# Expert matrices of a mixture-of-experts layer loaded whole, 2 MB at a time, in place of two halves of 1 MB

## What is computed

```python
def hier_moe(u, w_rg, b_rg, w_re, b_re, w_gate, w_up, w_down):
    g_prob = softmax(xf @ w_rg + b_rg);  g_val, g_idx = top_k(g_prob, 1)      # one of 4 groups
    top_v, top_i = top_k(e_in, MOE_TOPK)                                      # 2 of its 8 experts
    ...
    for g in range(MOE_GROUPS):
        h = silu(einsum('nd,edf->nef', xf, w_gate[g])) * einsum('nd,edf->nef', xf, w_up[g])
        out = out + einsum('nef,ne,efd->nd', h, combine[:, g], w_down[g])
```

## Time and profile before

| | us |
|---|---|
| median of 3 runs | 1304.13 |
| lowest, highest | 1302.29, 1308.63 |
| the profiled execution's own time | 1302.72 |
| its span, first to last instruction | 1300.9 |
| PE busy | 1243.2 |
| DVE busy | 912.5 |
| ACT busy | 682.3 |
| POOL busy | 286.4 |

### The profile page before, as it was taken

How to read it: one execution, slowest core, us unless ns; L and a number is a source line. 1 busy time by engine, 2 the same in 40 slices (tenths; PEclk the granted TensorE clock), 3 DMA queues, 4 the chain that set the end, 5 groups by cost and what they waited for, 6 DMA issues and landing times.

```text
span 1300.9 us, 16695 instructions
## 1 busy us (share of the span) xinstructions
PE 1243.2 (96%) x5716; PEld 919.0 (71%) x5716; DVE 912.5 (70%) x1046; ACT 682.3 (52%) x904; POOL 286.4 (22%) x202
## 2 busy tenths in 40 slices
PE   5999999999999999999999979999999999999997
PEld 3677877777898898888778756666666665666652
DVE  5878677742444333335789889789899988888875
ACT  2522554524333343345231448577888777777752
POOL 0101000000000000000010034346666653434430
PEclk9999999999999999999999989999999999999999
DMA  9985130312203214234262889999999999999963
GB/s 365 387 331 222 65 113 17 102 61 100 65 31 113 75 40 148 80 113 149 90 239 82 354 307 383 390 390 399 407 406 404 401 398 403 407 404 407 403 261 132
DMA packets 58471, 313.68 MB, mean 241 GB/s; under 512 B 10933, under 2 KB 11093, under 8 KB 31536
## 3 DMA queue, kind: packets, MB, share of 16 engines
q1 hardware_dynamic: 47536, 283.90, 55.8%
q0 software_dynamic: 10592, 27.99, 6.9%
q10 hardware_dynamic: 288, 1.05, 0.2%
HBM read 304.62 MB, written 20.49 MB: 250 GB/s over the span
## 4 chain that ended last, share of the span: by engine, by line
PE 73%; DMA 11%; DVE 10%; issue 3%; POOL 1%; ACT 1%; SPq 0%; DVEq 0%; POOLq 0%; ACTq 0%
PE ps L820 13%; PE ps L822 13%; PE ps L821 13%; PE ps L1074 6%; DMA w_raw<-in 6%; PE ps L1054 4%; PE ps L1055 4%; DVE w_lo L1775 3%; PE ps L951 2%; DMA xg<-u_d,ui 2%; DMA y_d<-yb,ui 2%; PE ps L997 2%; PE ps L1085 1%; PE ps L1087 1%; PE ps L1086 1%
## 5 line engine op out<-in xcount | busy, mean ns | idle before, releaser
L1775 DVE TENSOR_TENSOR w_lo<-w_raw,w_hi 128x2048 fp32r<-128x2048 f32 x159 | 362.8, 2285 | 39.0 <-ACT w_hi L1278 38.9
L1278 ACT CAST w_hi<-w_raw 128x2048 fp32r<-128x2048 f32 x159 | 300.1, 1907 | 55.3 <-DMA w_raw<-in 44.8
L1054 PE MATMUL ps<-w_hi,xT_all 128*128 128x512 f32 x464 | 191.7, 413 | 19.1 <-DVE w_lo L1775 14.1
L1055 PE MATMUL ps<-w_lo,xT_all 128*128 128x512 f32 x464 | 183.6, 396 | 0.0
L1467 DVE TENSOR_TENSOR d_lo<-d_raw,d_hi 128x1024 fp32r<-128x1024 f32 x96 | 114.8, 1221 | 73.9 <-ACT d_hi L1184 73.7
L820 PE MATMUL ps<-uT_hi,d_hi 128*128 128x512 f32 x384 | 154.5, 402 | 0.1
L822 PE MATMUL ps<-uT_hi,d_lo 128*128 128x512 f32 x384 | 149.9, 390 | 0.0
L821 PE MATMUL ps<-uT_lo,d_hi 128*128 128x512 f32 x384 | 149.7, 390 | 0.0
L742 POOL DMA_INDIRECT y_d<-yb,ui x31 | 112.0, 3614 | 146.4 <-DVE yb L1915 127.2
L1054 PEld LDWEIGHTS ps<-w_hi,xT_all 128*128 128x128 f32 x464 | 88.2, 190 | 49.9 <-DVE w_lo L1775 26.1
L1074 PE MATMUL ps<-w_raw,hT 128*80 128x512 f32 x264 | 118.5, 592 | 1.4 <-DVE yb L1915 1.4
(11 more groups left out here) (370 smaller groups left out, 2150.1 us busy)
## 6 DMA issues: line engine op xcount, KB each, us to landing
w_raw<-in SPq DMA_DIRECT2D x192, 1024.0 KB, 20.4
d_raw<-in SPq DMA_DIRECT2D x96, 512.0 KB, 3.6
ada_buf<-in SPq DMA_DIRECT2D x8, 2048.0 KB, 9.4
ada_w<-in SPq DMA_DIRECT2D x8, 1024.0 KB, 11.0
att_d<-Og POOLq DMA_DIRECT2D x2, 1056.0 KB, 7.7
O<-att_d POOLq DMA_DIRECT2D x2, 1056.0 KB, 8.0
x_in<-in SPq DMA_DIRECT2D x1, 2048.0 KB, 17.1
brep_d<-bvec_d POOLq DMA_DIRECT2D x2, 1024.0 KB, 26.7
```

The source lines that it names most:

```text
L1054: pe.matmul(bank(b), xT_all[s][:, k, :], hi[:, w], start=(k == 0), stop=False)
L1055: last = pe.matmul(bank(b), xT_all[s][:, k, :], lo[:, w], start=False, stop=(k == KD - 1))
L1278: act.copy(w_hi[n % NHI][:, :], w_raw[j][:, :]).then_inc(w_hi_rdy, 1)
L1775: dve.tensor_tensor(w_lo[j][:, :], w_raw[j][:, :], w_hi[n % NHI][:, :].bitcast(f32), ALU.subtract).then_inc(w_lo_rdy, 1)
```

## The change

SP now moves a whole matrix with one transfer of 2 MB, 16 KB in each partition, into two neighbouring slots (`w_mat`). The slots themselves, ACT's and DVE's splits and PE's products stay halves of 1 MB. A matrix is issued when *both* halves that held its two slots are used; both of its halves count as landed when the whole has landed. The expert loads become 96 in place of 192. There are six landing semaphores instead of twelve.

```diff
--- before.py
+++ after.py
@@ -191,7 +191,8 @@
 
     RAW_AT = (80, 88, 16, 24, 32, 40, 0, 8, 48, 56, 64, 72)
     HI_AT = (112, 120, 128, 136, 96, 104)
-    w_raw = [at(f"w_raw{n}", kb, [P, 2048]) for n, kb in enumerate(RAW_AT)]
+    w_mat = [at(f"w_raw{m}", kb, [P, 4096]) for m, kb in enumerate(RAW_AT[::2])]
+    w_raw = [w_mat[n // 2][:, 2048 * (n % 2):2048 * (n % 2) + 2048] for n in range(NRAW)]
     w_lo = [at(f"w_lo{n}", kb, [P, 2048], r32) for n, kb in enumerate(RAW_AT)]
     w_hi = [at(f"w_hi{n}", kb, [P, 2048], r32) for n, kb in enumerate(HI_AT)]
     FD = FF // P
@@ -458,7 +459,7 @@
         "ln_in", "u2_rdy", "u2_store", "u2T_ps", "u2T_sb", "logits_ps"))
     rt_ge, rt_gexp, rt_asg, rk_ps, oh_rdy, ids_ps, idx_rdy, tab_rdy, x1_rdy = (sem(n) for n in (
         "rt_gargs", "rt_gexp", "rt_assign", "rank_ps", "onehot_rdy", "ids_ps", "idx_rdy", "tab_rdy", "x1_rdy"))
-    w_in_sb = d_in + [sem(f"w_piece_in{n}") for n in range(SLOTS, NRAW)]
+    w_in_sb = d_in[0:NRAW // 2]
     w_hi_rdy, w_lo_rdy, w_used = sem("w_hi_rdy"), sem("w_lo_rdy"), sem("w_used")
     x1_st, x_hi, h_hi = (sem(n) for n in ("x1_store", "moe_x_hi", "moe_h_hi"))
     xg_in = [sem("xg_in0"), sem("xg_in1")]
@@ -519,8 +520,8 @@
 
     def landed(eng, n, i):
 
-        j = n % NRAW
-        slabs = len(range(j, 4 * len(items), SLOTS)) if j < SLOTS else 0
+        j = n % NRAW // 2
+        slabs = len(range(j, 4 * len(items), SLOTS))
         eng.wait_ge(w_in_sb[j], 16 * (i + (n // NRAW + 1 + slabs)))
 
     def splits(n, i):
@@ -575,36 +576,32 @@
             for r in ada_after.get(j, ()):
                 load_ada(r)
 
-        def piece(n, w, e, h, i=0):
+        def matrix(m, w, e):
 
             src = w[e] if isinstance(e, int) else w[bass.ds(e, 1)].rearrange("e p m -> (e p) m")
-            sp.dma_start(w_raw[n % NRAW][:, :], src[:, 2048 * h:2048 * h + 2048]).then_inc(w_in_sb[n % NRAW], 16)
+            sp.dma_start(w_mat[m][:, :], src).then_inc(w_in_sb[m], 16)
 
         sp.wait_ge(out_rdy, len(outs))
-        for n, (w, e) in enumerate(((w_gate, 0), (w_up, 0), (w_gate, 1), (w_up, 1), (w_down, 0), (w_gate, 2))):
-            for h in range(2):
-                piece(2 * n + h, w, e, h)
+        for m, (w, e) in enumerate(((w_gate, 0), (w_up, 0), (w_gate, 1), (w_up, 1), (w_down, 0), (w_gate, 2))):
+            matrix(m, w, e)
 
         def stage(i, s, w_next=True):
             c = 2 * i + s
             e, e1, e0 = (sp.value_load(tab_u[0:1, bass.ds(x, 1)], min_val=0, max_val=NE - 1) for x in (c, c + 1, c - 1))
             todo = [(w_up, e), (w_down, e0)] + ([(w_gate, e1)] if w_next else [(w_down, e)])
             for j, (w, x) in enumerate(todo):
-                for h in range(2):
-                    n = 6 * s + 2 * j + h
-                    sp.wait_ge(w_used, NRAW * i + n + 1)
-                    piece(n, w, x, h)
-
-        for j, (w, e) in enumerate(((w_up, 2), (w_down, 1))):
-            for h in range(2):
-                sp.wait_ge(w_used, NRAW + 2 * j + h + 1)
-                piece(2 * j + h, w, e, h)
+                m = 3 * s + j
+                sp.wait_ge(w_used, NRAW * i + 2 * m + 2)
+                matrix(m, w, x)
+
+        for m, (w, e) in enumerate(((w_up, 2), (w_down, 1))):
+            sp.wait_ge(w_used, NRAW + 2 * m + 2)
+            matrix(m, w, e)
         sp.wait_ge(tab_rdy, 1)
         last = last_pair(sp)
         e3 = sp.value_load(tab_u[0:1, 3:4], min_val=0, max_val=NE - 1)
-        for h in range(2):
-            sp.wait_ge(w_used, NRAW + 4 + h + 1)
-            piece(4 + h, w_gate, e3, h)
+        sp.wait_ge(w_used, NRAW + 6)
+        matrix(2, w_gate, e3)
         stage(1, 1)
         with sp.Fori(2, last) as i:
             stage(i, 0)
@@ -1275,7 +1272,7 @@
             landed(act, n, i)
             if not isinstance(i, int) or NRAW * i + n >= NHI:
                 act.wait_ge(w_used, NRAW * i + (n - NHI + 1 + NRAW))
-            act.copy(w_hi[n % NHI][:, :], w_raw[j][:, :]).then_inc(w_hi_rdy, 1)
+            act.copy(w_hi[n % NHI][:, :], w_raw[j]).then_inc(w_hi_rdy, 1)
 
         for kind, a in steps:
             if kind == "z":
@@ -1772,7 +1769,7 @@
 
             j = n % NRAW
             dve.wait_ge(w_hi_rdy, splits(n, i))
-            dve.tensor_tensor(w_lo[j][:, :], w_raw[j][:, :], w_hi[n % NHI][:, :].bitcast(f32),
+            dve.tensor_tensor(w_lo[j][:, :], w_raw[j], w_hi[n % NHI][:, :].bitcast(f32),
                               ALU.subtract).then_inc(w_lo_rdy, 1)
 
         def x_rest(c, s):
```

## The result

| | us |
|---|---|
| with the change, median of 4 runs | 1321.77 (1314.93 to 1338.71) |
| before, in the same comparison, median of 4 runs | 1303.71 |
| ratio | 1.0114, 95% interval 1.0061 to 1.0167 |
| the profiled execution's own time, its span | 1314.93, 1313.1 |
| the same, before | 1302.72, 1300.9 |

The kernel became slower by about 1.1%, as forecast in sign; the median lies 10 us above the forecast and inside its range, near its upper end of 1323. The ratio leaves out the one slow execution, 1338.71, and so is smaller than the quotient of the two medians. The two profiled executions differ by 12.2 us.

What follows compares the result with a forecast made beforehand. PE sets the pace first, the DMA stream later, with POOL's gather loop 0.5 us from binding. Late start plus gather delays, 1.6 + 3L and the loop, gave +7.8 on 1302.72, 1310.5; with the median 1.4 higher, 1312, range 1300 to 1323.

Steps and rivals of the forecast that it cites:

- Part 2: Start of the expert part: the whole first matrix lands later, +1.0 us on the path and +0.6 for the first gather.
- 3L: Chain up to 905.43 us: three gather or scatter landings, each later by L, delay PE.
- the loop: Two-chunk loop of yb, scatter, gather and PE's products: takes (30.0 + L)/2 us per chunk over 21 chunks.
- Part 5: POOL's gathers and scatters wait behind SP's larger packets; with the late start, +7.8 us in all.
- L: Extra landing time per gather or scatter on POOL: six waits of 0.30 us, 1.8 us, bounds 0 and 3.2.
- Part 3: Ring refills go in pairs: the queue loses at most 2.45 us once, early on; taken as +1.9 us.
- Part 1: Expert loads, 192 to 96 with 16 KB rows: stream no faster, taken as 0, between -5 and +5 us.
- Part 4: End of the expert part: both halves land together, so one more cast is paid once, +1.0 us.
- B: Rival, expert loop: gathers stay hidden, L below 1.56, the DMA path adds 4.5 us, 1308.6; chance 0.28.
- C: Rival, POOL's gathers: much later, from L = 2.3; at 2.4 us per wait +15.9, 1320.0; chance 0.15.
- D: Rival, late chunks: large rows give more bandwidth and gathers keep their margin, faster, 1291; chance 0.08.
- E: Rival, whole kernel: the ring absorbs everything, the start's delay included, 1304; chance 0.07.

Runs made afterwards that it cites:

- experiment two: The changed kernel with matrices laid half by half in DRAM, so each 2 MB transfer has 8 KB rows: 1316.62 us, ratio 1.0059.
- five: The changed kernel with 8 KB rows in its 2 MB transfers and POOL's gathers issued ahead of the scatters: 1315.38 us, ratio 1.0066.
- experiment one: The kernel before, still 1 MB loads with 8 KB rows, but SP waits for both halves before refilling: 1310.71 us, ratio 1.0040.
- experiment three: The changed kernel, 16 KB rows kept, with the gather of chunk c+3 issued ahead of the scatter of chunk c-1: 1314.36 us, ratio 1.0042.
- experiment nine: The kernel before, with whole-matrix 16 KB-row loads from the ring's third round on and gathers issued ahead of scatters: 1306.21 us, ratio 0.9995.
- ten: The kernel before, with whole-matrix 16 KB-row loads from the ring's third round on, gathers left behind the scatters: 1318.55 us, ratio 1.0074.
- experiment eight: The changed kernel run again without further edits: 1328.70 us, ratio 1.0137 to the kernel before.
- the hold: The changed kernel with SP's first refill held until the first gather lands: 1323.25 us, ratio 1.0108; with early gathers too, 1310.69 us, 1.0008.

## Why the prediction was right in sign, and where it was off

The profiled execution was forecast at 1310.5 and took 1314.93. Here is the sum of +7.8 for it beside the +12.2 by which the two spans differ:

| | forecast | measured |
|---|---|---|
| up to chunk 1 (Part 2) | 1.6 | 6.1 |
| chunk 1 to 10 (3L) | 5.4 | 3.2 |
| chunk 10 to 31 (the loop) | 0.8 | 5.8 |
| last stage | 0 | -2.9 |

So the total came nearer than its terms: two were too small, and two errors of the other sign, 2.2 and 2.9 us, hid half of that. This much is luck.

**Part 5, the mechanism, holds.** Six waits of 0.30 us were to make a gather L = 1.8 us later. Against the 8.7 us of the earlier trace rows the landings from chunk 10 on are 10.3, L = 1.6; at equal order on POOL 1.3. Outside that stretch L is larger. From 800 to 905 us the medians are 8.8 before and 12.3 with the change. Behind 1060 us they are 6.8 and 10.1: there the gathers' own time on POOL also stays at 2.77 us where before it fell to 0.99, in every kernel with 2 MB transfers, 8 KB rows included (2.77 us in experiment two, 2.97 in five), and not in experiment one (0.99). The turn of the loop, predicted at 30.0 + 1.8 = 31.8 us, reads 31.44 in the chain. PE's wait at line 1040 was to be 0.7 us a chunk and is 17.1 / 21 = 0.8. Experiments three and nine, and nine beside ten above all, show that the late gathers are what costs in the loop, by taking the wait away. The 21 chunks took 338.9 us, 16.14 each, where 15.9 was predicted (15.0 + 0.9); so this stretch lost 5.8 us against a predicted 0.8 (21 x 15.9 - 333.1).

**The loop's excess: a scatter that was not covered, and then the clock.** Part 5 put the scatter's own landing at nothing, as POOL waits 3.2 us for `yb` ahead of it. In two places it was not covered. The chain ahead of 932.92 is shown above. Ahead of 1174.22 the scatter of 1137.89 takes 12.83 us to land, POOL's copy of 128 numbers behind it (L728) takes 6.00 us where it takes 0.18 in all the other turns from chunk 11 on, and so the next scatter (1158.22) and the gather behind it (1163.20, 10.97 us) come late. From transposes to transposes these two steps take 18.22 and 18.83 us, in place of 15.72; that is 5.6 us, lost before the clock fell. Why a copy of 0.18 us at times takes 4 to 6 is not tested. The long ones of the chain run beside DVE's subtractions and end with them (882.86 and 882.82, 899.58 and 899.52 us), so that DVE holds them up is likely.

Then the clock: the sum took PE's speed from windows at 1.00. Behind both idle times stands a stretch at 1.2 GHz, 0.77 over 15 us and 0.91 over 20 us, that is some 7 and 4 us at the lower level, and at most 3.5 and 2 us of PE's time. The steps that hold them take 17.63 and 16.53 us, 2.7 us in all above 15.72. That they come behind idle times of 3.12 and 3.72 us is what the rows show; that the idle time causes it is supported by the kernels with early gathers and 16 KB rows, whose three windows from 900 to 1200 us all have 1.00. Not every such idle time is followed by it: after 2.93 us at 1021.18 in experiment eight the clock stays at 1.00 up to 1035.

How often this happens differs between executions. Experiment eight's, with five long waits for two, has a loop longer by 5.9 us. By the slopes above, a mean clock of 0.983 in place of 0.990 goes with some 7 us (an estimate). The forecast had no term for it, and it makes up much of the 10 us between forecast and median; what lowers the clock outside the loop stays open.

**Part 2 was mis-sized.** ACT's first cast was to end at 730.0; it ended at 729.8, and `u2T` came at 729.66 as forecast at about 730. But the first gather, to which I gave +0.6 of 0 to 2, took 11.5 us in place of 7.4. POOL's timeline:

```profile
759.73 2.13 POOL L719 DMA_INDIRECT xg<-u_d,ui  x1 [25.96 <-DVE wtab L1886]
...
767.52 1.00 POOL L719 DMA_INDIRECT xg<-u_d,ui  x1 [0.98 <-POOL ui L728]
```

Issued at 759.73 (before 757.80), it is followed at 760.28 by SP's first refill, of 2 MB; PE starts at 771.32. In the kernel before the refill had been issued at 754.74. So the chunk-1 transposes were 6.1 late, not 1.6: 4.1 from the landing, 1.9 from the issue. Of the latter Part 2 explains a third, since `u2T` came 0.63 us later than before; the rest stays open. Experiment one gives +2.0 for the gather with pairing and 8 KB rows, the hold removes it whole.

**Part 3's +1.9 was low as well.** I bounded the pairing by one half's transfer, 2.45 us. Experiment one has 1.0040, 4 to 5 us, since its refills are also issued right behind the first gather (759.83 after 759.28) and delay it; my bound treated the queue alone and not whom it delays. That it is a matter of the first rounds was right: pairs from the third round on cost nothing once the gathers are early (experiment nine).

**Part 1's 0 held for the total, with a trend below it.** In the three windows from 900 to 1200 us the early-gather kernels with 16 KB rows move 408, 407, 407 GB/s (experiment three) and 411, 408, 407 (nine), the kernel before 406, 402, 405; with 4 KB rows it is 397, 394, 394. A gain of up to 1% is there in experiment nine and too small to show in its time. Part 4's +1.0 cannot be read: the end of the changed kernel does not stand on a landing of `w_raw`, and the last stage gave 2.9 us back.

**The rivals.** B (gathers hidden) falls in the changed kernel: PE waits 17.1 us at line 1040 and the cast 4.0. With early gathers it is what happens: 1.0042, against the 4.5 us, or 1.0035, of its sum (experiment three), and the cast waits for `w_raw` again (34.2 us from 905 to 1240). C (gathers much later, 2.4 us per landing) gave 1320.0, nearer to the median than the forecast. From chunk 10 on it does not hold: none of the 21 gathers lands later than 11.0 us. Ahead of chunk 10 it does: the six from 800 to 905 us land after 11.4 to 13.2 us, 3.5 more than before in the median, 2.9 at equal order on POOL. So C was right for one stretch and wrong for the longer one. The Trainium skill ("DMA: Bandwidth & Descriptors", Queues, rings and completion order) would have an engine take turns by packets of some 9 to 17 descriptors. The trace bears that out in part at most: from chunk 10 on the growth of 1.3 to 1.6 us for a doubled row fits four or five more waits of 0.30 us per gather, ahead of it 2.9 fits about ten, and no row shows how large a turn is. D (faster) needed the gathers' margins to hold, and even where they do, experiments three and nine are no faster than before. E is out.

**No version beats the kernel before.** The best with whole matrices is experiment nine at 0.9995 (0.9968 to 1.0022), which cannot be told from it.

## What to carry to other kernels

A larger transfer on one queue is a longer wait for every small transfer of another queue on the same engines. Before enlarging it, find who waits for the small ones and with what margin; here 0.5 us of margin stood against 1.3 to 1.6 us of growth. Ask the same of the transfers behind which the small ones are issued: a scatter taken as covered was not, in some turns of the loop. If the large rows are wanted, first move the small transfers' issue ahead of whatever holds them, and keep the refills at the start of a pipeline small, where the queue isn't yet full.

## What the runs showed of the hardware

- Landing of a gather beside a full load stream, median, at equal order on POOL (experiments five and three): 9.0 us at 8 KB rows and 10.3 at 16 KB from chunk 10 on, 8.8 and 11.7 from 800 to 905 us.
- The first gather, from its issue to PE's transposes: 6.9 us with the refill held, 7.5 in the kernel before (refills of 1 MB, issued singly from 754.74 on), 8.2 beside a refill in rows of 4 KB, 9.1 to 9.7 in 8 KB, 11.3 to 11.9 in 16 KB.
- Stream beside the gathers, 900 to 1200 us, where gathers don't hold it up: 394 to 397 GB/s in rows of 4 KB, 402 to 407 in 8 KB, 406 to 411 in 16 KB. Going from 8 to 16 KB gives up to 1%, going down to 4 KB takes 2 to 3%.
- Idle times of TensorE of 3.12 and 3.72 us in an otherwise full loop were followed by stretches at 1.2 GHz, some 7 and 4 us long by the granted clock of 0.77 over 15 us and 0.91 over 20; an idle time of 2.93 us in experiment eight was not.
- Time of the kernel before against its mean granted clock: 1.02 to 1.09 us more for each 0.001 less, in three groups of 31, 25 and 21 runs.
